# Prompt attention's head-pair loop written out, and the first norm regrouped around a joint first up and gate tile

## What is computed

```python
def post_norm_ffn(x, mix, conv_prev, ln1_w, ln1_b, w_up, w_gate, conv_w, conv_b, w_down, ln2_w, ln2_b):
    h = layer_norm(ALPHA * x + mix, ln1_w, ln1_b)
    f, conv_new = conv_ffn(h, conv_prev, w_up, w_gate, conv_w, conv_b, w_down)
    return layer_norm(ALPHA * h + f, ln2_w, ln2_b), conv_new
```

## Time and profile before

| | us |
|---|---|
| median of 3 runs (2134.36 to 2139.96) | 2138.0 |
| the profiled execution | 2139.22 |
| its span, first to last instruction | 2137.5 |
| TensorE busy | 1989.5 (93%) |
| VectorE busy | 1159.1 (54%) |
| ScalarE busy | 648.8 (30%) |
| GpSimd busy | 218.8 (10%) |

### The profile page before, as it was taken

The page is one execution under the profiler, slowest core; times in us unless marked ns, Lnnn a source line. Parts: engine busy times, 40 slices in busy tenths (PEclk is TensorE's granted clock), DMA queues, the critical chain, the costliest instruction groups (busy, mean ns, idle before and its releaser), DMA issues.

```text
span 2137.5 us, 39105 instructions
## 1 busy us (share of the span) xinstructions
PE 1989.5 (93%) x14335; PEld 1861.5 (87%) x14335; DVE 1159.1 (54%) x1771; ACT 648.8 (30%) x1179; POOL 218.8 (10%) x253
## 2 busy tenths in 40 slices
PE   7898998899999899989898898799999999999996
PEld 5796896798898798878798897799999999999996
DVE  4554454977867867885424856533322333233348
ACT  4444343134133223213401103434301322132224
POOL 1000000020020020020000101300000000100004
PEclk9999999999999999989999999899999999999999
DMA  4211101787987878886732310111111111111144
GB/s 126 63 32 50 40 21 51 233 311 245 310 281 262 301 264 298 278 308 231 252 94 89 106 49 11 40 49 40 50 49 50 40 48 43 54 42 49 43 142 131
DMA packets 151682, 276.50 MB, mean 129 GB/s; under 512 B 19042, under 2 KB 57951, under 8 KB 151543
## 3 DMA queue, kind: packets, MB, share of 16 engines
q1 hardware_dynamic: 115970, 175.26, 24.4%
q0 software_dynamic: 23232, 82.80, 13.0%
q10 hardware_dynamic: 12368, 16.88, 2.1%
HBM read 247.24 MB, written 27.72 MB: 129 GB/s over the span
## 4 chain that ended last, share of the span: by engine, by line
PE 44%; DVE 5%; DMA 1%; issue 1%; ACT 1%; SPq 0%; DVEq 0%; ACTq 0%
PE bank L121 40%; PE bank L1670 3%; DVE x_lo L1898 1%; DMA gated_raw<-gated_t_scratch 1%; DVE chunk_tmp L1827 1%; DVE chunk_tmp L1829 0%; DVE z L1895 0%; DVE moving_lo L1833 0%; DVE merged_hi L1831 0%; PE banks L1628 0%; DVE w_lo L1968 0%; DMA tail_raw<-in_w_down_dram 0%; DVE y L1944 0%; DMA z<-fox_t_scratch 0%; PE banks L1656 0%
## 5 line engine op out<-in xcount | busy, mean ns | idle before, releaser
L121 PE MATMUL bank<-x_hi,w_hi 128*128 128x344 f32 (+1 forms) x1944 | 641.5, 330 | 44.4 <-DVE x_lo L1898 15.1
L121 PE MATMUL bank<-x_lo,w_hi 128*128 128x344 f32 (+1 forms) x1944 | 631.6, 325 | 0.0
L121 PE MATMUL bank<-x_hi,w_lo 128*128 128x344 f32 (+1 forms) x1944 | 631.3, 325 | 0.0
L121 PEld LDWEIGHTS bank<-x_hi,w_hi 128*128 128x128 f32 (+1 forms) x1944 | 372.4, 192 | 61.6 <-issue 48.6
L121 PEld LDWEIGHTS bank<-x_lo,w_hi 128*128 128x128 f32 (+1 forms) x1944 | 372.5, 192 | 1.6
L121 PEld LDWEIGHTS bank<-x_hi,w_lo 128*128 128x128 f32 (+1 forms) x1944 | 372.1, 191 | 1.7
L97 ACT ACTIVATE w_hi<-w_raw 128x1024 fp32r<-128x1024 f32 (+3 forms) x139 | 142.1, 1022 | 453.7 <-PE bank L121 419.5
L121 PE MATMUL bank<-moving_hi,w_hi 128*128 128x344 f32 x744 | 227.0, 327 | 13.7 <-DVE moving_hi L1806 7.0
L121 PE MATMUL bank<-moving_lo,w_hi 128*128 128x344 f32 x744 | 237.6, 319 | 0.0
L104 DVE TENSOR_TENSOR w_lo<-w_raw,w_hi 128x1024 fp32r<-128x1024 f32 (+3 forms) x139 | 164.4, 1182 | 103.2 <-ACT w_hi L97 101.4
L121 PE MATMUL bank<-moving_hi,w_lo 128*128 128x344 f32 x648 | 208.1, 321 | 0.0
(11 more groups left out here) (275 smaller groups left out, 2781.3 us busy)
## 6 DMA issues: line engine op xcount, KB each, us to landing
cache_keys<-in_cache_k_dram SPq DMA_DIRECT2D x256, 256.0 KB, 4.8
cache_vals<-in_cache_v_dram SPq DMA_DIRECT2D x256, 256.0 KB, 5.1
w_raw<-in_w_in_dram POOLq DMA_DIRECT2D x52, 512.0 KB, 6.3
w_raw<-in_w_up_dram POOLq DMA_DIRECT2D x22, 512.0 KB, 4.5
w_raw<-in_w_gate_dram POOLq DMA_DIRECT2D x22, 512.0 KB, 4.5
tail_raw<-in_w_down_dram SPq DMA_DIRECT2D x22, 448.0 KB, 3.9
gate<-gate_t_scratch SPq DMA_DIRECT2D x15, 516.0 KB, 3.5
w_raw<-in_w_down_dram POOLq DMA_DIRECT2D x10, 448.0 KB, 4.4
```

The source lines that it names most:

```text
L121: mm = pe.matmul(g.bank[n][0:m, 0:TC], w[slot][:, k, 0:m], x[:, k, chunk(n)], start=(k == 0 and i == 0), stop=(k == kt - 1 and i == 2))
```

## The change

1. In `fox` the loop of two passes is written out on all five engines, with constants in place of the loop's registers. The work and its order stay.
2. In `finish`, VectorE scales by the reciprocal only. ScalarE applies ln1_w and ln1_b in place on z, waits for that (`h_full`), and copies z rounded to x_hi. VectorE subtracts x_hi from z, in turns with its scaling of the next chunk.
3. The gate weight of the first tile is split early: on ScalarE after the squares of chunk 0, on VectorE between the first and second centring.
4. The first up and gate tile is taken out of the loops: for each chunk TensorE forms up and then gate, gate in banks 4, 5 and 7, and waits for x_lo one k tile at a time.
5. GpSimd issues the loads of the second tile's two weights before its scaling by ALPHA, which now has one constant and waits for x_lo of its chunk.

```diff
@@ -422,7 +422,7 @@
...
-                with pool.Fori(0, NIT) as it:
+                for it in range(NIT):
@@ -436,7 +436,7 @@
...
-                with sp.Fori(0, NIT) as it:
+                for it in range(NIT):
@@ -450,7 +450,7 @@
...
-                with pe.Fori(0, NIT) as it:
+                for it in range(NIT):
@@ -540,7 +540,7 @@
...
-                with act.Fori(0, NIT) as it:
+                for it in range(NIT):
@@ -624,7 +624,7 @@
...
-                with dve.Fori(0, NIT) as it:
+                for it in range(NIT):
@@ -1503,7 +1503,8 @@
...
             sem(n) for n in ("z_part", "z_done", "z_summed", "mean", "centred", "squared", "var", "root", "inv_root"))
-        normed, h_hi, h_lo, h_scaled = (sem(n) for n in ("z_normed", "h_hi", "h_lo", "h_scaled"))
+        normed, h_full, h_hi, h_lo, h_scaled = (sem(n) for n in ("z_normed", "h_full", "h_hi", "h_lo", "h_scaled"))
+        gate_bank = (g.bank[4], g.bank[5], g.bank[7])
         fc_done, c1, conv, gelu, a_hi, a_lo = (sem(n) for n in ("fc_done", "conv_first", "conv_step", "gelu", "a_hi", "a_lo"))
@@ -1579,12 +1580,14 @@
...
                         up_and_gate(0, f0, ju)
+                        up_and_gate(1, f0, ju)
                         for k in range(NCH):
-                            pool.wait_ge(normed, (k + 1) * KD)
+                            pool.wait_ge(h_full, (k + 1) * KD)
+                            pool.wait_ge(h_lo, (k + 1) * KD)
                             for t in range(KD):
-                                ins = pool.tensor_scalar(acc[:, t, chunk(k)], z[:, t, chunk(k)], ln_cols[:, 1, t:t + 1], ALPHA, ALU.add, ALU.mult)
+                                ins = pool.tensor_scalar(acc[:, t, chunk(k)], z[:, t, chunk(k)], ALPHA, None, ALU.mult)
                             ins.then_inc(h_scaled, 1)
-                    with pool.Fori(1 if s == 0 else 0, n) as i:
+                    with pool.Fori(2 if s == 0 else 0, n) as i:
                         up_and_gate(i, f0, ju)
@@ -1635,9 +1638,26 @@
...
                 var_of(2)
+                ju = sections[0][2]
+                up_job, gate_job = job(ju, ju % 2, 0), job(ju, ju % 2, 1)
+                pe.wait_ge(centred, NCH)
+                pe.wait_ge(root, 2)
+                for n in range(NCH):
+                    for (j, slot), dst in ((up_job, bank[n]), (gate_job, gate_bank[n])):
+                        pe.wait_ge(g.w_split, RING + j + 1)
+                        pe.wait_ge(g.bank_free[n], ju + 1)
+                        for k in range(KD):
+                            pe.wait_ge(h_lo, n * KD + k + 1)
+                            for q, (w, x) in enumerate(((g.w_hi, g.xh), (g.w_hi, g.xl), (g.w_lo, g.xh))):
+                                mm = pe.matmul(dst[:, 0:TC], w[slot][:, k, :], x[:, k, chunk(n)],
+                                               start=(k == 0 and q == 0), stop=(k == KD - 1 and q == 2))
+                        mm.then_inc(g.mm_chunk, 1)
+                pe.wait_ge(z_part, 2)
+                pe.wait_ge(g.bank_free[NCH - 1], ju + 2)
+                pe.transpose(bank[3][0:NS + 2, 0:P], up[:, SEQ:SEQ + NS + 2], g.ident[:]).then_inc(cr_t, 1)
                 for f0, n, ju, jd in sections:
-                    with pe.Fori(0, n) as i:
-                        product(g, pe, job(i * 2 + ju, ju % 2, 0), g.xh, g.xl, before=lambda k: pe.wait_ge(h_lo, (k + 1) * KD))
+                    with pe.Fori(0 if f0 else 1, n) as i:
+                        product(g, pe, job(i * 2 + ju, ju % 2, 0), g.xh, g.xl)
                         product(g, pe, job(i * 2 + ju, ju % 2, 1), g.xh, g.xl)
@@ -1718,9 +1738,12 @@
...
                         act.wait_ge(normed, n * KD + k + 1)
-                        act.activation(g.xh[:, k, chunk(n)], z[:, k, chunk(n)], ACT.Identity, bias=ln_cols[:, 1, k:k + 1]).then_inc(h_hi, 1)
+                        act.activation(z[:, k, chunk(n)], z[:, k, chunk(n)], ACT.Identity, scale=ln_cols[:, 0, k:k + 1], bias=ln_cols[:, 1, k:k + 1]).then_inc(h_full, 1)
+                        act.wait_ge(h_full, n * KD + k + 1)
+                        act.activation(g.xh[:, k, chunk(n)], z[:, k, chunk(n)], ACT.Copy).then_inc(h_hi, 1)
                 act.wait_ge(ln_land, 32)
                 squares(0)
+                split_hi(g, act, job(JF, JF % 2, 1))
                 squares(1, range(0, 3))
@@ -1730,23 +1753,28 @@
...
                 h_high(2)
-                act.wait_ge(h_lo, NCH * KD)
                 act.wait_ge(z_part, 2)
                 for s, (f0, n, ju, jd) in enumerate(sections):
-                    with act.Fori(0, n) as i:
+                    def tile(i, first):
                         f = i + f0
-                        split_hi(g, act, job(i * 2 + ju, ju % 2, 1))
+                        if not first:
+                            split_hi(g, act, job(i * 2 + ju, ju % 2, 1))
                         act.wait_ge(conv, f * 5)
...
                         for k in range(NCH):
-                            chunk_ready(g, act, i * 2 + ju, k)
+                            if first:
+                                act.wait_ge(g.mm_chunk, NCH * (RING + ju) + 2 * k + 1)
+                            else:
+                                chunk_ready(g, act, i * 2 + ju, k)
                             act.activation(up[:, 2 + k * TC:2 + (k + 1) * TC], bank[k][:, 0:TC], ACT.Copy).then_inc(g.bank_free[k], 1)
...
                         act.activation(act_in[:, 0:SEQ], up[:, 0:SEQ], ACT.Identity, scale=fc[:, 16:17], bias=fc[:, 19:20]).then_inc(c1, 1)
+                        if first:
+                            act.wait_ge(g.mm_chunk, NCH * (RING + ju) + 2 * NCH - 1)
                         split_hi(g, act, job(i * 2 + ju, ju % 2, 2))
@@ -1758,6 +1786,11 @@
...
                         act.activation(cr, bank[3][0:NS + 2, 0:P], ACT.Copy).then_inc(cr_out, 1)
+
+                    if s == 0:
+                        tile(0, True)
+                    with act.Fori(1 if s == 0 else 0, n) as i:
+                        tile(i, False)
 
@@ -1884,24 +1917,38 @@
...
                     dve.tensor_tensor(z[:, :, chunk(n)], z[:, :, chunk(n)], wide_chunk(bank[3 + n][:, 0:TC]), ALU.subtract).then_inc(centred, 1)
-                for n in range(NCH):
-                    centre(n)
-                for n in range(NCH):
+                centre(0)
+                split_lo(g, dve, job(JF, JF % 2, 1))
+                centre(1)
+                centre(2)
+                dve.memset(up[:, 0:2], 0.0).then_inc(z_part, 1)
+
+                def invert(n):
                     dve.wait_ge(root, n + 1)
...
 
+                def scale(n, k):
+                    dve.tensor_tensor(z[:, k, chunk(n)], z[:, k, chunk(n)], rstd[:, chunk(n)], ALU.mult).then_inc(normed, 1)
+
+                def h_low(n, k):
+                    dve.wait_ge(h_hi, n * KD + k + 1)
+                    dve.tensor_tensor(g.xl[:, k, chunk(n)], z[:, k, chunk(n)], g.xh[:, k, chunk(n)].bitcast(F32), ALU.subtract).then_inc(h_lo, 1)
+                invert(0)
+                for k in range(KD):
+                    scale(0, k)
+                for n in range(NCH):
+                    if n < NCH - 1:
+                        invert(n + 1)
                     for k in range(KD):
-                        dve.scalar_tensor_tensor(z[:, k, chunk(n)], z[:, k, chunk(n)], ln_cols[:, 0, k:k + 1], rstd[:, chunk(n)], ALU.mult, ALU.mult).then_inc(normed, 1)
-                    for k in range(KD):
-                        dve.wait_ge(h_hi, n * KD + k + 1)
-                        dve.scalar_tensor_tensor(g.xl[:, k, chunk(n)], z[:, k, chunk(n)], ln_cols[:, 1, k:k + 1],
-                                                 g.xh[:, k, chunk(n)].bitcast(F32), ALU.add, ALU.subtract).then_inc(h_lo, 1)
-                dve.memset(up[:, 0:2], 0.0).then_inc(z_part, 1)
+                        h_low(n, k)
+                        if n < NCH - 1:
+                            scale(n + 1, k)
                 for s, (f0, n, ju, jd) in enumerate(sections):
-                    with dve.Fori(0, n) as i:
+                    def tile(i, first):
                         f = i + f0
-                        split_lo(g, dve, job(i * 2 + ju, ju % 2, 1))
+                        if not first:
+                            split_lo(g, dve, job(i * 2 + ju, ju % 2, 1))
                         dve.wait_ge(a_lo, f)
@@ -1918,11 +1965,19 @@
...
                         for k in range(NCH):
-                            chunk_ready(g, dve, i * 2 + ju + 1, k)
-                            dve.tensor_tensor(act_in[:, chunk(k)], act_in[:, chunk(k)], bank[k][:, 0:TC], ALU.mult).then_inc(g.bank_free[k], 1)
+                            if first:
+                                dve.wait_ge(g.mm_chunk, NCH * (RING + ju) + 2 * k + 2)
+                            else:
+                                chunk_ready(g, dve, i * 2 + ju + 1, k)
```

(6 more changed lines are left out.)

## The result

| | before | after |
|---|---|---|
| median of 5 runs, us | 2138.0 (2134.36 to 2140.91) | 2116.9 (2114.68 to 2123.07) |
| profiled execution, its span | 2139.22, 2137.5 | 2117.18, 2115.2 |
| ratio | | 0.9904, 95% interval 0.9885 to 0.9924 |

That is 21.1 us less, against a forecast of 13 with a range that ended at 2118. A repeat of the after kernel gave 2114.62 (0.9898, 0.9883 to 0.9914), a third run 2116.85 (0.9918, 0.9902 to 0.9935).

What follows compares the result with a forecast made beforehand. TensorE, busy 93% of the span, was taken as the bound, so only its waits and half clock counted. Attention's 7.1 us and the norm's 5.7 made 12.8, forecasting 2125 us, own range 2120 to 2130, range asked for 2118 to 2134.

Steps and rivals of the forecast that it cites:

- Everything after attention follows in sequence and moves along: After attention: later stages only start earlier by what attention gains; no gain of their own was counted.
- The stop, 4.2 us: Attention, between second and third pair: TensorE's pause, put down to its taken branch, falls from 5.16 to 0.92 us.
- Clock behind it, 2.9 us: Attention's third pair: less half clock after the pause gives back 2.1 to 3.7 us, middle taken.
- Front of the norm: First norm's start: the early gate weight split moves the first reciprocal from 1320.9 to 1324.9; second root at 1331.7.
- ScalarE carries the norm: First norm: ScalarE sets the pace, 24 tiles at 1.16 us; VectorE's last subtraction at 1360.6, 3.9 later than before.
- Second tile 6.7 earlier, minus 1 for the clock: Feed-forward's second tile starts at about 1368.1, 6.7 us earlier; 1 subtracted for low clock; sum 5.7 (0 to 9.5).
- VectorE came true in part: Rival in the first norm: VectorE, slowed beside GpSimd, bounds it; 4.6 us lost, about 2130 us; 12%.
- The half clock in the joint tile: Rival: TensorE stays at half clock through the joint up and gate tile; total gain 3 to 7, about 2133; 13%.
- Written-out code: Rival in attention: new TensorE code arrives haltingly, 5 to 7 us per halt; about 2148 us with four; 4%.
- At nothing: Around the norm: earlier weight loads, GpSimd's scalings ending near 1368, the moving_hi copy's wait and saved table loads count nothing.
- VectorE losing 14.1 us by that rule: Rival in the first norm: GpSimd's port lock blocks VectorE fully, 14.1 us added, about 2139 us; 3%.

Runs made afterwards that it cites:

- the seven: Seven profiles of kernels that keep TensorE's attention loop; retention takes 936.1 to 945.4 us, mean 940.0.
- the ten: Ten profiles of kernels with TensorE's attention loop written out; retention takes 932.6 to 936.3 us, mean 934.0.
- pe_only: The before kernel with the attention loop written out on TensorE alone: 2124.7 us, ratio 0.9942 to before.
- all_but_pe: The before kernel with the attention loop written out on the four other engines and kept on TensorE: 2135.7 us, ratio 0.9989 to before.
- pe_loop_kept: The after kernel with the attention loop put back on TensorE alone: 2130.1 us, ratio 0.9971 to before.
- split_late: The after kernel with the first gate weight split later, on ScalarE after the second root, on VectorE after chunk 0's first scaling: 2116.1 us, ratio 0.9906 to before.
- second_tile: The after kernel with the second tile also out of TensorE's loop and its up weight split before the first tile's convolution: 2113.8 us, ratio 0.9889 to before.
- fill_after: The after kernel with 72 more small transposes on TensorE behind the attention loop: 2126.1 us, ratio 0.9941 to before.

## Why the prediction was wrong

The direction, what the two edits do and the order of the two gains were right. The time was 1.1 us below the range: 21 us gained where 12.8 stood. Means over the profiles, kept against changed: attention 318.0 (seven) and 308.9 (ten), retention 940.0 and 934.0, norm 87.9 (seven) and 80.6 (seven). That is 9.1 + 6.0 + 7.3 = 22.4 us, against 7.1 + 0 + 5.7.

- **"Everything after attention follows in sequence and moves along"** is the step that failed. It counted the untouched retention stage at nothing; in the profiles it became about 6 us shorter. Nothing in the forecast had a place for it, neither the sum nor a rival nor the range. The 6.0 is an upper figure: the profiled executions of the seven lie on average 3.6 us above their kernels' medians, those of the ten 0.7 below. By medians the loop is worth 11 to 15 us, which beside attention's 9.1 leaves 2 to 6. The two terms that were sized too small (2.0 in attention, 1.6 in the norm) had their part as well: with any one of the three right, the time would have been inside the range.
- **The stop, 4.2 us:** right. Expected 0.92, measured 0.69 (4.5 gained; 4.3 on average). It is TensorE's branch, shown by pe_only, all_but_pe and pe_loop_kept. The Trainium skill's figure of 108 ns (Advanced Engine Details and Errata, Control Flow Timing) doesn't hold for this branch of 4119 ns. Another rule of the Trainium skill does fit: a taken branch whose target is out of the fetched window has to fetch it first (Runtime: NRT & Kernel Launch, Instruction fetch mechanics). The traces agree with the 16 KB of instructions that come inside each of the eight branches, and with the short loop's branch at L1639, which took 208 ns.
- **Clock behind it, 2.9 us:** right in size for the third pair, 77.8 to 74.7 on average, 3.1 (in the first two profiles 78.30 to 74.53, 3.8, just over the upper bound of 3.7). What the sum left out, on average: 0.6 us in the second pair, 0.6 in the fourth, and 0.5 at the other boundaries, where 0.88 to 0.92 became 0.69. The fourth pair's 76.23, which stood in the forecast as a measure of a good pair, was itself slow; the seven have a median of 74.8 there, the ten 74.4.
- **Front of the norm:** right. The first reciprocal was forecast at 1324.9 and came at 1309.15 + 16.01 = 1325.2; ScalarE's first Identity at 1331.7, and came at 1314.73 + 16.01 = 1330.7, the lower of the two bounds.
- **ScalarE carries the norm:** right for the first chunk and for the time of the last x_lo, and mis-sized by its wait for itself: 0.1 forecast, 0.03 measured, 24 times. A k tile took 1.09 instead of 1.16, and the last x_lo came at 1358.0 instead of 1360.6. But in the second chunk VectorE set the pace, and in the third TensorE, which was still busy with the second. Up ended at 1343.06 + 16.01 = 1359.1 instead of 1361.2.
- **Second tile 6.7 earlier, minus 1 for the clock:** 8.6 earlier, minus 1.8 for the clock (24.59 against 22.77). The mechanism, the gate multiply that frees the bank, is the row at 1349.62. Net 6.8 against 5.7 in this pair of profiles.
- **Rivals.** VectorE came true in part. Beside GpSimd five of its eight x_lo of the second chunk took 0.78 instead of 0.50, one x_lo and one scaling took it 1.13 us against ScalarE's 1.09, and for 11 us it was the chain. It cost little, as it caught up in the third chunk: with x_lo in step with ScalarE up would have ended at about 1342.6 instead of 1343.06 (an estimate from the last x_lo, 1341.95, and three matmuls). The half clock in the joint tile didn't come: TensorE went from var into it at full clock after 0.57 us, and being fed 3 matmuls per 1.09 us didn't bring the clock down. (In split_late, behind 2.61 us, it did start at half clock.) Written-out code brought no new stop, as the boundaries at 0.69 show, which agrees with what the forecast took from the Trainium skill on sequential fetch (Runtime: NRT & Kernel Launch, Instruction fetch mechanics).
- **At nothing:** held. GpSimd's scalings ended at 1353.6 (1369.6 in before's time, forecast 1368) and made the moving_hi copy wait 4.19 us; TensorE didn't notice. GpSimd's 24 scalings took 27.7 us instead of 21.2: in the new form one starts 1.04 us after the other even with VectorE out of the way (0.53 in the old), and 1.13 beside it.

VectorE's subtraction beside GpSimd and without it, from second_tile's timeline, the first still under GpSimd's scaling:

```profile
1334.94 0.78 DVE L1949 TENSOR_TENSOR x_lo<-z,x_hi 128x344 fp32r<-128x344 f32 x1
1335.64 0.50 DVE L1945 TENSOR_TENSOR z<-z,stage 128x344 f32<-128x344 f32 x1
1336.07 0.50 DVE L1949 TENSOR_TENSOR x_lo<-z,x_hi 128x344 fp32r<-128x344 f32 x1
```

The Trainium skill (SBUF — State Buffer, SBUF: two separate sides) has the loser of the shared ports blocked fully. The forecast gave 3% to VectorE losing 14.1 us by that rule, and that didn't come: a lost turn cost it 0.28 us, on one of the two operations of a k tile. But it read the row at 3.98 of the earlier trace rows wrongly as speaking against a full block. GpSimd's timeline of before over the same stretch shows who lost:

```profile
1340.11 4.23 POOL L1585 TENSOR_SCALAR acc<-z,ln_cols 128x344 f32<-128x344 f32 x1 [6.69 <-DVE z L1895]
```

This one scaling, which takes 0.55 us undisturbed, lasted until VectorE's eight x_lo had ended (1339.93 + 3.98 = 1343.9), and VectorE ran at its full pace meanwhile. That agrees with the rule.

## What to carry to other kernels

Look at TensorE's own branch rows before believing the engine that a wait is put down to: the long loop body here cost 4 us per taken branch plus the clock behind it, and writing out that one list was enough. When a stop on the busiest engine goes, measure the stages behind it too. Judge the gain from several profiles cut into stages, since a stage that nobody touched moved here by nearly as much as each edit, and hold the profiled executions against the medians, since a profile can be of a long execution. A stretch taken as the undisturbed yardstick must itself be shown undisturbed. An operation that looks slow by its mean may be one that was held once for long, as GpSimd's scaling was: look at least, median and most.

## What the runs showed that was not expected

- The first product of retention comes after a stop of 2.7 us that is put down to TensorE's own queue. It is none of TensorE's: the engines meet there, and the last to come is SyncE, which waits for the store of the last pair. In after it issues that store at 356.51 and goes on at 359.2:

```profile
356.51 0.34 SPq L446 DMA_DIRECT2D fox_t_scratch<-fox_t  x1
```

```profile
L422 SPq COMPARE_BRANCH  x1: 38/38/38, 359.2 to 359.2; - x1
```

```profile
359.93 0.40 PE L121 MATMUL bank<-x_hi,w_hi 128*128 128x344 f32 x1 [2.71 <-PEq L422]
```

  When 72 short transposes were queued ahead, TensorE worked through this wait and the stop was 0.96. TensorE's timeline in fill_after:

```profile
359.57 5.63 PE L535 MATMUL banks<-ident,logf 8*128 8x8 f32 x81 [0.69 <-DVE fox_t L666]
366.16 0.62 PE L121 MATMUL bank<-x_hi,w_hi 128*128 128x344 f32 x1 [0.96 <-PEq L422]
```

- ScalarE's wait for its own previous result costs 0.03 us between Identity and Copy, where it is the only wait, and 0.24 at L1749, which has several (0.16 for the same instruction in after). That the number of waits makes the difference isn't shown.
- Stops of similar length were followed by different losses of clock: 4.8 to 5.9 us with the branch by 2.3 to 3.9 us in the next pair (against 74.4), 5.28 us without it by 1.4; and at the second tile 3.29 us by 1.8 us, 3.06 us by 0.3. What decides between them, no run here shows.
